# Neighbourhood attention regrouped into tiles of 8 rows by 16 columns, two heads a step, with dense products beside every step

## What is computed

```python
r0 = jnp.clip(r - kh // 2, 0, rows - kh)            # kh = 8, rows = 16
col_start = np.clip(c - NA_KW // 2, 0, GRID_W - NA_KW)   # NA_KW = 16, GRID_W = 64
sc = jnp.einsum('bjqhd,bkjchd->bhjqkc', qb, k_band) * scale
sc = jnp.where(mask, sc + bias, -jnp.inf)           # bias by row and column distance
p = jax.nn.softmax(sc, axis=(-2, -1))
o = jnp.einsum('bhjqkc,bkjchd->bjqhd', p, v_band)
o_b = o * jax.nn.silu(g_b)
```

## Time and profile before

| | us |
|---|---|
| median of 3 runs | 2111.5 (2109.32 to 2118.55) |
| the profiled execution | 2119.89 |
| its span, first to last instruction | 2118.1 |
| the stage of the change | 390.8 to 777.7, so 386.9 |
| PE busy in the span | 2002.0 (95%) |
| DVE, ACT, POOL busy | 1088.5, 822.6, 406.3 |

### The profile page before, as it was taken

One profiled execution on the slowest core, in us unless ns is written; L12 is line 12 of the kernel. 1 busy time (PEld: TensorE's weight loads), 2 busy tenths in 40 slices (PEclk: granted clock), 3 DMA queues, 4 the chain that ended last, 5 costly groups with the idle time before them and its releaser, 6 DMA issues.

```text
span 2118.1 us, 40035 instructions
## 1 busy us (share of the span) xinstructions
PE 2002.0 (95%) x16753; PEld 1705.6 (81%) x16753; DVE 1088.5 (51%) x2458; ACT 822.6 (39%) x1726; POOL 406.3 (19%) x404
## 2 busy tenths in 40 slices
PE   7988999999999999998999999999999999999997
PEld 6987778788888899996777777777777777887897
DVE  4767877325615662602445444454444366875503
ACT  5346777322223232422333333433334245444423
POOL 2540000121040003222123222121222120001211
PEclk9999999998999999999999999999999999999999
DMA  4102000310030032233221121122211220003441
GB/s 170 41 21 39 2 1 1 75 41 1 16 80 21 1 120 81 83 93 94 68 77 53 56 72 54 56 64 76 61 56 58 69 75 21 11 21 139 140 149 80
DMA packets 123432, 128.97 MB, mean 61 GB/s; under 512 B 29209, under 2 KB 108757, under 8 KB 123253
## 3 DMA queue, kind: packets, MB, share of 16 engines
q1 hardware_dynamic: 123173, 125.91, 19.4%
q0 software_dynamic: 80, 0.50, 0.1%
HBM read 93.83 MB, written 33.63 MB: 60 GB/s over the span
## 4 chain that ended last, share of the span: by engine, by line
PE 72%; DVE 6%; ACT 4%; POOL 2%; issue 1%; DMA 1%; SPq 0%; DVEq 0%; POOLq 0%; ACTq 0%
PE ps L988 8%; PE ps L990 6%; PE ps L989 6%; PE ps L670 6%; PE ps L672 6%; PE ps L671 6%; PE ps L1091 4%; PE ps L1275 3%; PE ps L813 3%; PE ps L1298 3%; PE ps L1128 3%; PE ps L801 2%; PE ps L1285 1%; PE ps L758 1%; PE ps L1157 1%
## 5 line engine op out<-in xcount | busy, mean ns | idle before, releaser
L2757 POOL TENSOR_TENSOR t<-t,t 128x512 fp32r<-128x512 f32 x183 | 238.0, 1315 | 1010.3 <-ACT t L1376 991.2
L670 PE MATMUL ps<-t,t 128*128 128x256 f32 (+2 forms) x1264 | 394.5, 312 | 5.7 <-DVE t L2725 2.0
L671 PE MATMUL ps<-t,t 128*128 128x256 f32 (+2 forms) x1264 | 390.8, 309 | 0.0
L672 PE MATMUL ps<-t,t 128*128 128x256 f32 (+2 forms) x1264 | 390.7, 309 | 0.0
L988 PE MATMUL ps<-t,t 128*128 128x512 f32 (+2 forms) x720 | 299.1, 415 | 1.4 <-ACT t L1652 1.4
L990 PE MATMUL ps<-t,t 128*128 128x512 f32 (+2 forms) x720 | 269.9, 375 | 0.0
L989 PE MATMUL ps<-t,t 128*128 128x512 f32 (+2 forms) x720 | 269.3, 374 | 0.0
L670 PEld LDWEIGHTS ps<-t,t 128*128 128x128 f32 x1264 | 243.9, 193 | 18.7 <-issue 5.7
L671 PEld LDWEIGHTS ps<-t,t 128*128 128x128 f32 x1264 | 243.8, 193 | 10.8 <-issue 0.2
L672 PEld LDWEIGHTS ps<-t,t 128*128 128x128 f32 x1264 | 243.6, 193 | 10.8
L988 PEld LDWEIGHTS ps<-t,t 128*128 128x128 f32 x720 | 136.5, 190 | 30.4 <-issue 4.5
(11 more groups left out here) (271 smaller groups left out, 3735.7 us busy)
## 6 DMA issues: line engine op xcount, KB each, us to landing
t<-in_w_in SPq DMA_DIRECT2D x37, 512.0 KB, 5.9
t<-in_w_in SPq DMA_DIRECT2D x14, 1024.0 KB, 5.3
zgate_spill<-t SPq DMA_DIRECT2D x20, 512.0 KB, 3.2
t<-in_x SPq DMA_DIRECT2D x16, 512.0 KB, 8.3
t<-zgate_spill SPq DMA_DIRECT2D x16, 512.0 KB, 3.6
feat_spill<-t SPq DMA_DIRECT2D x13, 512.0 KB, 3.3
t<-feat_spill SPq DMA_DIRECT2D x39, 128.5 KB, 3.0
t<-in_w_out SPq DMA_DIRECT2D x4, 1024.0 KB, 5.1
```

Source lines behind the costliest of these rows:

```text
L670: e.matmul(dst, lh, rh, start=k == 0, stop=False)
L671: e.matmul(dst, lh, rl, start=False, stop=False)
L672: m = e.matmul(dst, ll, rh, start=False, stop=k == n - 1)
L2757: e.tensor_tensor(WLO[wslot(b)][:, o], WST[:, o], WHI[wslot(b)][:, o].bitcast(F), ALU.subtract).then_inc(w_lo.sem, w_lo.up((b, p)))
```

## The change

Queries are grouped into 8 tiles of 8 grid rows by 16 columns. All of a tile's windows lie in 12 rows by 32 columns (384 keys). A step takes one tile and two heads. The key rows are read from `KH`/`KL` with a stride (`band_keys`), and q is stored in tile order by ACT and DVE (`by_band`, `banded`). The heads' scores alternate between the upper and the lower 64 partitions and go to two banks. For the values the stationary operand is 128 keys x 64 value columns, once per head, writing to partitions 0 to 63 and 64 to 127 of one bank. The output comes out turned, ACT copies it, and PE turns it back (`band_output`).

v and gates of two heads share a weight block. They go from PSUM to a staging tile (`VGS`), to DRAM (`vg_d`), and come back arranged by band (`VBAND`, 16 DMAs) and by tile (`GBP`, 8 DMAs). The stage goes over four pairs of heads `p`: 4 q and k results of 24 products, then 8 steps; beside each step stands one v-and-gate result of the next pair (24 products), for the last pair one turn of the mixed result. The bias is prepared in DRAM (`band_d`: one fill and 40 small DMAs, issued before full attention) and loaded by 32 DMAs a pair into two tiles.

```diff
-        for h in range(2):
-            for c in (1280 + 256 * h, 1792 + 256 * h, 2304 + 256 * h, 2816 + 256 * (1 - h)):
-                wplan.append(([w1[:, c:c + 256]], 8, 256))
+        for h in range(4):
+            for c in ((2304, 2816), (1280, 1792)):
+                wplan.append(([w1[:, c_ + 128 * h:c_ + 128 * h + 128] for c_ in c], 8, 256))
...
+        def band_keys(t, buf, pr):
+            return buf[pr, :].rearrange("p (r c) -> p r c", c=64)[:, 4 * (t // 4):4 * (t // 4) + 12, BAND[t % 4]:BAND[t % 4] + 32]
... PE
+            def values_and_gates(p, i, hi, lo, choice):
+                ps = bank(("vg", p, i), choice, (v_out, (p, i)), (mixed_v, ("gate", 8 * p + i)))
+                by_tokens(ps[:, 0:256], i, hi, lo, 8, ("vg", p, i))
+            def band_scores(m):
+                for x, (q, k) in enumerate(((QH, KH), (QL, KH), (QH, KL))):
+                    for s in range(2):
+                        pr = slice(64 * s, 64 * s + 64)
+                        mm = e.matmul(pss[s][:, 0:384], q[pr, tile128(t)], band_keys(t, k, pr), start=x == 0, stop=x == 2)
+            def band_turn(m):
+                for s in range(2):
+                    ps = bank_at(("t", m, s), 4 + s, (prob_hi, (m, s)))
+                    w.wait_ge(*prob[m, s])
+                    for k in range(3):
+                        mm = e.transpose(ps[:, tile128(k)], PBN[m % 3][s][:, tile128(k)], ident)
+            def band_value(m):
+                w.wait_ge(*d_vb[m // 8 - 8])
+                w.wait_ge(*prob_hi[m, 1])
+                for k in range(3):
+                    for s in range(2):
+                        mm = e.matmul(ob[64 * s:64 * s + 64, 0:128], VBAND[:, 4 * (t % 4) + t // 4 + k, 64 * s:64 * s + 64],
+                                      PBN[m % 3][s][:, tile128(k)], start=k == 0, stop=k == 2)
+            def band_output(m):
+                w.wait_ge(*value_t[m])
+                mm = e.transpose(ob[:, 0:128], OTB[m % 2][:, :], ident)
+            for p in range(4):
...             # 4 q and k results (banks 7, 0, 1, 7), the pair before's last turns, values and outputs between
+                for n in range(8):
+                    m = B_Z + 8 * p + n
+                    if n > 2:
+                        band_output(m - 3)
+                    band_scores(m)
+                    if n:
+                        band_turn(m - 1)
+                    if n > 1:
+                        band_value(m - 2)
+                    if p < 3:
+                        values_and_gates(p + 1, n, hi, lo, (7,))
+                    else:
+                        turn_mixed(n, 0, 7)
... ACT, in step n: band_turned(m - 1) twice, band_value(m - 2), band_prob(m) twice, values_and_gates or mixed_part
+            def band_turned(m):
+                    e.activation(PBN[m % 3][s][:, :], psum(("t", m, s))[:, 0:384], ACT.Copy)
+            def values_and_gates(p, i):
+                if z > 3:
+                    w.wait_ge(*d_vgs[z % 4][z - 4])
+                e.activation(VGS[z % 4][:, 0:128], psum(("vg", p, i))[:, 0:128], ACT.Copy, scale=0.5)
+                e.activation(TG[z % 2][:, :], psum(("vg", p, i))[:, 128:256], ACT.Tanh, scale=0.5)
... DVE, in step n: band_output(m - 3), band_row(m) twice, gate or mixed_part
+            def band_row(m, s):
+                e.tensor_tensor(row, psum(("s", m, s))[:, 0:384], band_bias(t, s), ALU.add)
+                maximum(row, 2 * m + s, (m, s))
+            def band_output(m):
+                e.reciprocal(RIN[:, c:c + 2], RSM[:, c:c + 2])
+                for s in range(2):
+                    e.scalar_tensor_tensor(out=MIXB[:, t, ...], in0=psum(("o", m))[:, hs], scalar=RIN[:, c + s:c + s + 1], in1=GBP[:, t, hs], ...)
... POOL: memsets of the two bias tiles at the start of the stage; no mask additions
... SP
+            def load_biases(p, r):
+                if p:
+                    w.wait_ge(*attn_v[B_Z + 8 * p - 5 + 4 * r, 1, "biased"])
+                for s in range(2):
+                    for q in range(8):
+                        e.dma_start(BIAS[r][16 * q:16 * q + 16, s, :, o:o + 256], ...)   # 48 KB each
+            def load_values_and_gates(p):
+                for z in range(8 * p + 4, 8 * p + 8):
+                    w.wait_ge(*d_vgs[z % 4][z])
+                if p:
+                    w.wait_ge(*value_mm[B_Z + 8 * p - 1])
+                ... 16 DMAs to VBAND, then wait for attn_v[B_Z + 8 * p - 1, 1, "out"], then 8 DMAs to GBP
+            for r in range(2):
+                load_biases(0, r)
+            for i in range(NT):
+                store_values_and_gates(0, i)
+            for p in range(4):
+                wt.enter()
+                load_values_and_gates(p)
+                if p < 3:
+                    wt.enter()
+                    for n in range(8):
+                        store_values_and_gates(p + 1, n)
+                        if n == 4:
+                            load_biases(p + 1, 0)
+                    load_biases(p + 1, 1)
```

More of the change, by code:

```diff
@@ L783, in paired @@
                         between(n)
[L786 to L830, removed]
             def scores_a(item, ps, z):
@@ L865, in pe_program @@
             PE.end("attention a")
-            for hh in range(2):
-                for what in "qk":
-                    hi, lo = enter()
[L871 to L875, removed]
-                    wt.leave()
[L877 to L914, removed]
-                        m.then_inc(score_mm.sem, score_mm.up(z))
-                    def values(item, k):
-                        _, h, i, inner = item
-                        w.wait_ge(*v_out[hh, NT - 1])
-                        return VB[:, window(i, inner)[1] // 128 + k, 64 * h:64 * h + 64]
-                    attention(FIRST_Z["b", hh, inner], B_ITEMS[hh, inner], lambda item: [128] * 4 + ([64] if item[3] else []),
-                              scores, values, (SBN, SBN), between, (6, 6))
-                for _ in gate_parts:
-                    pass
-                wt.leave()
-                PE.end(("attention b", hh))
@@ L940, in pe_program @@
+            for x in range(3):
+                band_output(B_Z + 29 + x)
+                if x == 0:
+                    band_turn(B_Z + 31)
+                if x < 2:
+                    band_value(B_Z + 30 + x)
+                    for t in (2 * x, 2 * x + 1):
+                        turn_mixed(t, 1, 2 * x + t % 2)
+            PE.end("attention b")
+            for t in range(4, NT):
+                turn_mixed(t, 1, None)
             PE.end("mixed turned")
@@ L2242, in dve_program @@
+            for x in range(3):
+                band_output(B_Z + 29 + x)
+                for t in (2 * x, 2 * x + 1) if x < 2 else ():
+                    mixed_part(t, 1)
+            DVE.end("attention b")
+            for t in range(4, NT):
+                mixed_part(t, 1)
             for q in EVERY:
-                w.wait_ge(*q["attention b", 1])
-            for g in range(2):
-                for i in range(NT):
-                    tile_rest_part("m", i, g)
+                w.wait_ge(*q["attention b"])
@@ L2806, in pool_program @@
                 wt.leave()
[L2807 to L2808 removed]
             POOL.end("attention a")
[L2812 to L2822 removed]
+            for q in EVERY:
+                w.wait_ge(*q["attention a"])
@@ L2834, in pool_program @@
-                gate_parts = gate_work()
-                for inner in range(2):
-                    if inner:
-                        w.wait_ge(*DVE["biases", hh])
-                        w.wait_ge(*POOL.last)
-                        e.memset(BI[64:128, :, 2, :], NEG).then_inc(bias_p.sem, bias_p.up(("rows0", hh)))
-                        w.wait_ge(*bias_p["rows0", hh])
-                        e.memset(BI[0:64, :, 10, :], NEG).then_inc(bias_p.sem, bias_p.up(("rows", hh)))
-                        w.wait_ge(*bias_p["rows", hh])
-                    for n in range(0, 18, 2):
-                        for _ in range(4):
-                            next(gate_parts, None)
```

525 lines of the change are left out of this document (269 added, 256 removed).

## The result

The changed kernel took 2135.74 us (median of 5, 2129.88 to 2139.72) and the kernel before 2116.88 (median of 5, 2109.32 to 2122.07): ratio 1.0094, 95% interval 1.0062 to 1.0125. I had forecast 2033 and a faster kernel; it is slower, by more than the 0.5% that can be told from no change. The profiled execution after took 2139.72, its span 2137.9.

The account below looks back on a forecast made before the run. PE, busy for 95% of the span, was taken as the bound. The stage's terms summed to 308.3 us against 386.9, 78.6 less, giving 2033; the range for 8 of 10 was 2008 to 2072.

Parts of the forecast that it names:

- SP and the loads: Prediction's step on SP's issues and DMA landings: stores, biases and band loads hidden, the staging wait costing PE 1 us.
- The preparation of the bias goes into the 270 us before 390 in which SP only fetches weights.: Ahead of the stage: claimed that preparing the bias fits into SP's free time, with no cost in the sum.
- In a pair SP issues ... 27 us of a pair's 66.: Within each pair of heads: SP's stores and loads take 27 of 66 us, band values arriving at 18, wanted at 33.
- The borders of 9 us: Gaps around the q and k products: 1.1 x 3 for bank 7, 1.5 x 4 before a pair's first scores.
- SP's issues become the bound: Rival: bias and band loads at 1.34 us an issue delay PE by 100 us, making 2133; chance 0.06.
- seven steps of the last pair: Attention steps without dense products: 5.3 us each, paced by DVE's chain, with PE idle for 2.2.
- last step and tail: End of the stage: after the last step the last rows, exponentials and turns run in series, 4 us for the tail.
- clock: Allowance for lowered PE clock in the stage: 6 us, with one possible fall in the last pair and the tail.
- The filled step: Each of 24 attention steps with dense products beside it: 5.5 us, set by PE, which doesn't wait.
- the halves overlap: Assumed side by side for scores and values, 2.6 us a step; rival of serial halves: 3.7, making 2068, chance 0.12.
- DVE and ACT don't pace the filled steps: Forecast put DVE at 3.4 and ACT at 3.6 us; rival that they pace: 24 us more, 2057, chance 0.10.
- The profiled execution's own time of 2119.9 becomes ...: Whole kernel: the stage's gain of 78.6 us taken off the profiled time gives 2041.3; the median is 8.4 lower.

Follow-up runs that it names:

- e1: Kernel before plus only the bias-table fill (5760 pieces of 128 B from one DRAM address), read by nobody: 2160.19 us, ratio 1.0242.
- e4: Changed kernel with the bias table filled from an SBUF tile in 640 pieces of 1152 B: 2091.31 us, ratio 0.9907 to the kernel before.
- e7: e6 with ACT's share of the next weights' split moved behind each q or k result: 2051.19 us, ratio 0.9684 to the kernel before.
- e5: Changed kernel with SP fetching the next weights ahead of the second 16 bias loads: 2103.11 us, ratio 0.9948 to the kernel before.
- e8: e6 with the first head's score and value products ahead of the second's: 2068.18 us, ratio 0.977 to the kernel before.
- e3: Kernel before plus a fill listed as 5760 pieces of 128 B, read from 5760 consecutive addresses: 2126.12 us, one run.
- e9: Kernel before plus a fill of the same bytes from one address in 640 pieces of 1152 B: 2113.94 us, one run.
- e2: As e1, with the fill written as 128 rows of 45 pieces: 2157.45 us, one run.
- e6: Changed kernel with both edits of e4 and e5: 2057.13 us, ratio 0.9756 to the kernel before.

## Why the prediction was wrong

**The step that failed** is "SP and the loads": it put the preparation of the bias and the loads of a pair at nothing, and left out who waits for the weights behind them.

- *"The preparation of the bias goes into the 270 us before 390 in which SP only fetches weights."* SP did have the time: it waited 80.8 us and nobody waited for SP. I priced the fill by SP's time and asked no one what the transfer itself does: how long 5760 pieces take, and whom else it holds up. It holds up PE, and with it the others. Price: 43.9 us between the starts of the stage in the two traces, 46.3 with the fill alone (e1), 44.4 by taking it away (e4). No row of before shows such a transfer, so here the range had to hold a bound, and held none.
- *"In a pair SP issues ... 27 us of a pair's 66."* The sum counts, but not the order. I followed the band values, for which no engine of the stage is seen to wait, and the staging tile (ACT waits 14.6 us for it instead of 4, and still the first scores of e7 come 0.8 us sooner than forecast), and not the next weights, which stand behind 16 bias loads. I had also taken 0.40 us for an issue; those of the bias take 11.45 / 16 = 0.72. A queue that is 40% full still delivers late what is asked for last: 32.6 us (e5).
- *ACT's tick ahead of the first copy of k.* The borders of 9 us had only what follows from PE's results. That a wait for weights stands ahead of that copy in ACT's order was missing: 5.9 us (e7).

The first and the second are 77 of the 103 us between 2033 and 2135.74. The rival "SP's issues become the bound" was on the right engine and forecast 2133, near the result, but by another mechanism: it wanted 1.1 us an issue and a wait for staging buffers, and the issues took 0.72. The wait for staging buffers cost PE nothing to be seen (46.6 us to the first scores, forecast 47.4), and no engine is seen to wait for the band loads. That its number fits is chance.

**The sum by its terms.** e7 is the changed kernel without the three. Its stage runs from 389.6 to 703.2, 313.6 against the forecast 308.3:

| stretch | forecast | e7 | after |
|---|---|---|---|
| start to first scores | 1 + 23.0 + 21.9 + 1.5 = 47.4 | 46.6 | 46.6 |
| three pairs, score to score | 3 x (8 x 5.5 + 21.9 + 2.6) = 205.5 | 220.2 | 263.1 |
| seven steps of the last pair | 7 x 5.3 = 37.1 | 30.2 | 29.5 |
| last step and tail | 5.3 + 4 + 4 = 13.3 | 16.7 | 16.7 |
| clock | 6 | in the rows | in the rows |

(Rounded, the forecast terms add up to 309.3. Here 21.9 is four results of 24 products at 0.2275, 2.6 a border of 1.1 + 1.5, and the two 4 in the tail the mixed turns left over and the tail's own 4. The stage after starts at 434.71. The first scores of the pairs stand at 436.16, 510.00, 582.26 and 656.31 in e7, at 481.27, 569.86, 657.88 and 744.40 after; the last ones at 686.54 and 773.85.)

- The filled step was right to 0.01 us: 5.51. With it fall two rivals: the halves overlap (scores in twos, values 0.88 against 1.14 in e8), and DVE and ACT don't pace the filled steps. That two sums of its parts were rounded up (2.44 to 2.5 and 3.61 to 3.7) changes nothing, since 2.6 was taken.
- The borders were too small. Three pairs are 14.7 longer in e7 than the terms give, 4.9 each. PE's timeline of e7 over the first of them shows what I had and what I hadn't:

```profile
478.37 0.47 PE L682 MATMUL ps<-t,t 128*128 128x512 f32 x1 [0.95 <-DVE t L2144]
486.18 0.88 PE L864 MATMUL ps<-t,t 128*64 128x128 f32 x12 [1.31 <-DVE t L2168]
494.79 0.88 PE L864 MATMUL ps<-t,t 128*64 128x128 f32 x12 [1.96 <-DVE t L2168]
510.00 0.80 PE L846 MATMUL ps<-t,t 64*128 64x384 f32 x6 [1.50 <-DVE t L2192]
```

  The first and the last wait are my 1.1 and 1.5, measured 0.95 and 1.50. The two in the middle are new: the values of a pair's last two steps stand between the q and k products, and their bank comes free only when DVE has read the output before out of it (L2168), which stands in DVE's order behind its copies of those products, and those wait for ACT's. The same four waits recur at each of the three borders: 1.31 + 1.96 = 3.3 of the 4.9. The clock takes 1.7 more in the first and in the third border (0.83 from 490 to 500 and from 640 to 650) and nothing in the second, 1.1 on average. Some 0.5 a pair is left over.
- The last pair was mis-sized the other way: 4.7 in its later steps and 30.2 / 7 = 4.3 on average instead of 5.3, with 1.25 us idle instead of 2.2. My likely mistake is that I put nearly all of ACT's and DVE's work of a step in a row. The last step and the tail took 3.4 more than forecast. In the sum the last pair and the clock's 6 us hid the borders. The Trainium skill says in "TensorEngine Tiling (Array Packing)", PSUM Bottleneck, that tiling doesn't speed up the emptying of PSUM. The trace agrees where nothing else fills PE: the value products wait 1.25 us in the step shown of the last pair for DVE to free their bank, and not at all in the filled steps.
- *"The profiled execution's own time of 2119.9 becomes ..."* assumed that all behind the stage stays. It is 1347.5 us in e7 and 1347.4 after, against 1340.4: 7 us more in both. Most of it isn't the change's: e3, which is the kernel before behind the stage, takes 1346.4 there, with the low clock from 1920 to 1940. After has such a stretch too (0.83 from 1930 to 1950), and e7 (0.66 from 1850 to 1860).

With 5.3 more for the stage and 7.1 behind it the forecast 2033 becomes 2045; e7 is at 2051.19 beside a kernel before of 2115.63, 4 above the median from which I started. So the sum of the stage came out within 5.3 us, in part because errors of its terms cancel, and the time was lost where the prediction didn't calculate.

**What stays open:** why reads of one address are so slow (a single DMA engine doesn't fit e9, whose DMA share is 0.51 from 124 to 130, well above 1/16); that it is the fetch of PE's instructions which they hold up (seen in the packets of two queues, not tested by itself); why the clock is lower at the borders of e8; and the rest of the borders.

## What to carry to other kernels

A DMA that "only" prepares data is hidden if nobody waits for its queue *and* if it leaves the memory and the DMA engines free; 5760 pieces read from one address didn't. It looks like this: PE idle with releaser "issue", the others waiting for PE, and the DMA share at 0.05. What helped here was to fill from SBUF (e4) or in few pieces of 1152 B (e9). Count the packets on the page, too: a list of 5760 pieces can turn out to be a few large ones (e3). And for loads that are moved, work out the landing of everything that is queued behind them, down to the engine in whose order the arrival is awaited, not only the sum of the issues.

## What the runs showed of the hardware

- 5760 pieces of 128 B from one address in DRAM take 80.8 us, 14 ns each and 9 to 10 GB/s (after, e1, e2); 640 pieces of 1152 B from one address start 13 ns apart too and land after 13.0 us (e9). 7680 pieces of 256 B from many addresses land after 18.5 us, 2.4 ns each (before).
- A list of pieces that follow one another on both sides went as 32 packets, not 5776 (e3).
- While the 5760 pieces last, PE stands still for 47.77 us (e1: 45.57), and the others wait for it, in a kernel too in which no engine of that stretch waits for the transfer. The granted clock falls to 0.50 in it, the lower level of 1.2 GHz.
- Value products of two 64-column halves of the array, issued in turn, take 0.88 us for 12 records; one half after the other 1.14 (e8). Score products of two 64-row halves run two at once in either order, 0.74 us for six (e6, e8).
- An issue on SP took 0.72 us for a bias load of 48 pieces of 1 KB, against 0.40 for weights.
